# RWKV chain ahead of attention in the first block of a two-block float32 kernel, with sigmoids written as tanh

## The reference

```python
h = rms_norm(x, pre_norm_gain)
proj = h @ w_in                                   # 1024 -> 8832 columns
# attention: 3 groups of 8 heads (q, k, v of 1536 columns each), dilations 1, 4, 16
num, den, mx = dilated_group_attention(q_g, k_g, v_g, bias_g, window, dilation)
o_attn = sum(w * num) / sum(w * den)              # merged over the groups: 512 columns
y_attn = (o_attn * silu(z_attn)) @ w_up_attn      # 512 -> 1024
# RWKV: r, k, v of 512 columns, w_low and a_low of 64 columns
pr = pr + (pr_prev - pr) * shift_mix              # token shift
w_log = -softplus(-(w0 + tanh(w_low) @ w_up)) - 0.5
decay = exp(-exp(w_log))                          # = exp(-e^-0.5 * sigmoid(...))
a = sigmoid(a0 + a_low @ a_up)
kk = normalised per head(k * k_k);  k = k * (1 + (a - 1) * k_a)
S = S * decay + (S @ -kk) (kk * a)^T + v k^T;  y = S @ r     # per token, 8 heads of 64
o_rwkv = group_norm(y) + bonus
y_rwkv = (o_rwkv * silu(z_rwkv)) @ w_up_rwkv      # 512 -> 1024
merged = sigmoid(g_attn) * y_attn + sigmoid(g_rwkv) * y_rwkv
x = x + rms_norm(merged @ w_out, post_norm_gain)
# then block two and the experts: 3 matrices of 1024 x 2816 for each of 16 experts
```

## Time and profile before

| | us |
|---|---|
| median of 3 runs | 2008.4 |
| the profiled execution, its own time | 2008.44 |
| its span in the trace | 2006.5 |
| start of the first projection tile | 17.20 |
| end of the 30 q, k, v tiles | 141.84 |
| first logits to last values of attention | 145.3 to 254.1 |
| end of the chain's last matmul | about 433.8 |
| start of `out1` | 486.55 |
| experts' stretch, DMA-bound | from about 780 to the end |

### The profile page before, as it was taken

One profiled execution on the slowest core, in us unless ns is written; L12 is line 12 of the kernel. 1 busy time (PEld: TensorE's weight loads), 2 busy tenths in 40 slices (PEclk: granted clock), 3 DMA queues, 4 the chain that ended last, 5 costly groups with the idle time before them and its releaser, 6 DMA issues.

```text
span 2006.5 us, 22014 instructions
## 1 busy us (share of the span) xinstructions
PE 1447.0 (72%) x10234; PEld 799.2 (40%) x10234; DVE 538.2 (27%) x696; ACT 162.8 (8%) x322; POOL 12.7 (1%) x25
## 2 busy tenths in 40 slices
PE   7999998887999879665656655656566656565655
PEld 6857877775485444221212222212122222121221
DVE  1005576854633532111111111011111110111112
ACT  2112130001210220000000000000000000000001
POOL 0000000001000000000000000000000000000000
PEclk9999998868999978787777877877878777778778
DMA  8342231114231659999999999999999999999996
GB/s 310 142 148 91 75 117 44 44 43 161 84 126 44 272 230 430 429 431 431 431 435 433 433 430 431 430 432 431 432 434 434 430 432 430 430 432 433 433 432 266
DMA packets 49342, 629.86 MB, mean 314 GB/s; under 512 B 2746, under 2 KB 3869, under 8 KB 36388
## 3 DMA queue, kind: packets, MB, share of 16 engines
q1 hardware_dynamic: 46464, 619.19, 73.3%
q0 software_dynamic: 2224, 8.17, 1.2%
q10 hardware_dynamic: 564, 1.10, 0.2%
HBM read 627.37 MB, written 1.09 MB: 313 GB/s over the span
## 4 chain that ended last, share of the span: by engine, by line
DMA 53%; PE 38%; DVE 7%; ACT 1%; issue 1%; ACTq 0%; DVEq 0%
DMA arena<-in_w_down 18%; DMA arena<-in_w_gate 18%; DMA arena<-in_w_up 16%; PE psum L793 10%; PE psum L1258 6%; PE psum L1300 3%; PE psum L1092 3%; PE psum L795 2%; PE psum L1016 1%; PE psum L1155 1%; DVE arena L1453 1%; PE psum L919 1%; PE psum L812 1%; PE psum L841 1%; PE psum L1006 1%
## 5 line engine op out<-in xcount | busy, mean ns | idle before, releaser
L1258 PE MATMUL psum<-arena 128*32 128x352 f32 x4096 | 415.5, 571 | 273.3 <-DMA arena<-in_w_gate 137.2
L1300 PE MATMUL psum<-arena 128*32 128x512 f32 x1408 | 236.7, 788 | 183.3 <-DMA arena<-in_w_down 180.3
L1258 PEld LDWEIGHTS psum<-arena 128*32 128x32 f32 x4096 | 152.1, 133 | 529.4 <-issue 221.5
L793 PE MATMUL psum<-arena 128*128 128x256 f32 x976 | 226.4, 389 | 1.0 <-ACT arena L540 0.6
L1300 PEld LDWEIGHTS psum<-arena 128*32 128x32 f32 x1408 | 65.7, 135 | 350.0 <-issue 249.9
L793 PEld LDWEIGHTS psum<-arena 128*128 128x128 f32 x976 | 186.2, 194 | 33.3 <-issue 4.8
L1804 DVE TENSOR_TENSOR arena<-psum,arena 128x1024 f32<-128x1024 f32 x30 | 36.7, 1225 | 408.6 <-PE psum L1310 408.6
L1787 DVE COPY arena<-psum 128x256 f32<-128x256 f32 x16 | 6.8, 425 | 303.2 <-PE psum L1286 303.2
L1796 DVE TENSOR_TENSOR arena<-psum,arena 128x704 f32<-128x704 f32 x16 | 14.3, 892 | 259.6 <-PE psum L1258 259.6
L743 ACT ACTIVATE arena<-psum 128x1024 f32<-128x1024 f32 x15 | 15.4, 1025 | 780.3 <-PE psum L1300 780.3
L1792 DVE RECIPROCAL arena<-arena 128x704 f32<-128x704 f32 x16 | 72.9, 4554 | 0.5
(11 more groups left out here) (368 smaller groups left out, 1147.9 us busy)
## 6 DMA issues: line engine op xcount, KB each, us to landing
arena<-in_w_gate SPq DMA_DIRECT2D x32, 5632.0 KB, 46.4
arena<-in_w_up SPq DMA_DIRECT2D x31, 5632.0 KB, 45.9
arena<-in_w_down SPq DMA_DIRECT2D x30, 5632.0 KB, 47.5
arena<-in_w_in SPq DMA_DIRECT2D x24, 2048.0 KB, 8.2
arena<-in_w_out SPq DMA_DIRECT2D x4, 2048.0 KB, 7.9
arena<-in_w_down SPq DMA_DIRECT2D x2, 2816.0 KB, 27.0
arena<-in_w_up SPq DMA_DIRECT2D x1, 4224.0 KB, 12.2
arena<-bias_rows POOLq DMA_DIRECT2D x3, 1024.0 KB, 8.7
```

The lines of the kernel that those rows point to most:

```text
L793: last = mm(o, block_of(blk)[:, k, c * P:c * P + P], rhs[:, k, :], start=(k == 0), stop=(k == KC - 1))
L1258: last = mm(psum[32 * j:32 * j + CAP, b + n, 0:HALFQ], XC[e % 2][:, k, :], region(o, HALFQ), start=(k == 0), stop=(k == KC - 1))
L1300: last = mm(psum[32 * g:32 * g + CAP, 4 + n, :], HT[:, i, :], region(spot(pos), 512), start=(i < 4), stop=(i >= FPP - 4))
```

## The change

The order of the first block is turned round. The blocks of weights are loaded, and the tiles computed, in the order low, k, r, v of RWKV, then q, k, v of attention, then the two silu gates, then the four merge gates. With it:

- The decay and key preparation runs beside the tiles of r, k, v and of q. Whole tiles, two per level, stand among the `pairs`; 3 whole and 8 half tiles (tiles 34 to 40) stand in the chain; six tiles cover the group norm, and four more cover its gating.
- Attention comes last. The 16 merge-gate tiles stand among its units, none behind the last one. The gating of a head (`gated`) is done on DVE straight from PSUM, where ACT copied it before.
- `w_up_rwkv` comes ahead of `w_up_attn`. The merge is one DVE operation per product and one add per k, on which `out1` waits step by step (`mg_ready`).
- Sigmoids are 0.5 * (1 + tanh(x / 2)): Tanh on ACT, and the rest folded into operations of two scalars on DVE. The eight reciprocals go, that of the key norm stays. The factor 0.5 of the merge is in the copy of `out1`.
- The last level's second set of `pairs`, which nothing read, is gone.
- POOL: the three bias loads wait for the last level (`T1_mm` 5). Of the ten loads after the group norm, `dist` and `lam` wait for the last logits and `w3` for the last maximum of attention, since their places in memory are in use until then.
- Buffers are placed anew.

```diff
-        blocks = [(f"q{i}", in_cols(w_in, 512 * i)) for i in range(3)]
+        blocks = [("low", in_cols(w_in, OFF_LOW, P))]
+        blocks += [(f"rkv{i}", in_cols(w_in, OFF_RWKV + 512 * i)) for i in (1, 0, 2)]
+        blocks += [(f"q{i}", in_cols(w_in, 512 * i)) for i in range(3)]
...
             def bank_of(j):
-            if j < ATT_TILES:
-                return j % 4
-            return 6 if PREP_TILE <= j < NORM_TILE and (j - PREP_TILE) % 2 else 7
+            if j < 2:
+                return 2 + j
+            return 6 + j % 2 if j < G_TILE else 7
...
+            pool.wait_ge(S["T1_mm"], 5)
             for g in range(NG):
...
+            pool.wait_ge(S["neg_max"], NU)
+            pool.dma_start(w3[0:64, :], A["filt_w3"]).then_inc(S["f_in"], 16)
...
-                    act.activation(dst, src, ACT.Exp, scale=-1.0).then_inc(S["proj_evac"], 1)
+                if j >= G_TILE:
+                    act.activation(dst, src, ACT.Tanh, scale=scale).then_inc(S["proj_evac"], 1)
...
             for lev in range(5):
                 pe.wait_ge(S["MM_done"], 2 * lev + 2 if lev else 3)
                 pairs(0, mOff, mMT).then_inc(S["T1_mm"], 1)
-                project(LEVEL_TILE + lev, 0, 4)
+                project(24 + 2 * lev)
                 pe.wait_ge(S["T1_done"], lev + 1)
                 pe.wait_ge(S["MM_done"], 2 * lev + 3)
                 pairs(2, mM, mT1).then_inc(S["MM_mm"], 1)
-                pairs(4, mT1, mM).then_inc(S["MM_mm"], 1)
-                project(LEVEL_TILE + lev, 4, 8)
+                if lev < 4:
+                    pairs(4, mT1, mM).then_inc(S["MM_mm"], 1)
+                project(25 + 2 * lev)
...
+            solve(0)
+            project(34)
+            step(0)
+            project(35)
+            state_parts(1)
+            project(36)
+            solve(1)
+            project(37, 0, 4)
+            step(1)
+            project(37, 4, 8)
+            state_parts(2)
+            project(38, 0, 4)
...
+            for j in range(41, 47):
+                project(j)
+            pe.wait_ge(S["gn_done"], 1)
...
+            for n in range(NU):
+                turned(n)
+                if n + 2 < NU:
+                    logits(n + 2)
+                if n + 1 < NU:
+                    project(G_TILE + 1 + n)
+                values(n)
...
-            link(V.tensor_scalar(LD, LD, 1.0, None, ALU.add))
-            link(V.reciprocal(LD, LD))
-            link(V.tensor_scalar(LD, LD, -E_HALF, None, ALU.mult))
+            link(V.tensor_scalar(LD, LD, -0.5 * E_HALF, -0.5 * E_HALF, ALU.mult, ALU.add))
...
-                if lev == 0:
-                    gate_group(0)
```

More of the change, by code:

```diff
@@ new lines, in _ @@
+            evac(0)
+            act.wait_ge(S["low_in"], 1)
+            act.activation(prT[0:64, 12, :], prT[0:64, 12, :], ACT.Tanh).then_inc(S["low_t"], 1)
+            evac(1)
+            evac(2)
+            act.wait_ge(S["low_mm"], 1)
+            for f in range(FT):
+                act.activation(LD[:, f, :], psum[:, f // 2, (f % 2) * T:(f % 2) * T + T], ACT.Tanh, scale=0.5,
+                               bias=small[:, 16 + f:17 + f])
+                last = act.activation(AA[:, f, :], psum[:, 2 + f // 2, (f % 2) * T:(f % 2) * T + T], ACT.Tanh, scale=0.5,
+                                      bias=small[:, 20 + f:21 + f])
@@ L543, in _ @@
+            evac(39)
+            evac(40)
+            evac(41)
+            act.wait_ge(S["mean_in"], 2)
+            act.activation(small[:, 64:80], small[:, 64:80], ACT.Sqrt).then_inc(S["root_in"], 1)
+            for j in range(42, 47):
+                evac(j)
+            act.wait_ge(S["gn_done"], 1)
+            for j in range(47, G_TILE):
                 evac(j)
@@ new lines, in _ @@
+            project(2)
+            pe.wait_ge(S["low_t"], 1)
+            pe.wait_ge(S["proj_evac"], 2)
+            for f in range(FT):
+                mm(psum[:, f // 2, (f % 2) * T:(f % 2) * T + T], lowW[0:64, f * P:f * P + P], prT[0:64, 12, :], start=True, stop=True)
+                last = mm(psum[:, 2 + f // 2, (f % 2) * T:(f % 2) * T + T], lowW[64:128, f * P:f * P + P], prT[64:128, 12, :], start=True, stop=True)
+            last.then_inc(S["low_mm"], 1)
+            for j in range(3, 9):
+                project(j)
@@ new lines, in _ @@
+            pe.wait_ge(S["sq_ready"], 1)
+            for f in range(FT):
+                last = mm(psum[:, 4 + f // 2, (f % 2) * T:(f % 2) * T + T], BLK1, TMP[:, f, :], start=True, stop=True)
+            last.then_inc(S["norm_mm"], 1)
+            for j in range(9, 18):
+                project(j)
+            pe.wait_ge(S["sq_ready"], 2)
+            pe.wait_ge(S["norm_sqrt"], 1)
+            for a in range(TT):
+                for f in range(FT):
+                    last = mm(psum[:, 4, a * 8 + 2 * f:a * 8 + 2 * f + 2], CS[:, f, a * P:a * P + P], small[:, 24 + 2 * f:26 + 2 * f], start=True, stop=True)
@@ L800, in _ @@
+            solve(3)
+            project(40, 0, 4)
+            step(3)
+            project(40, 4, 8)
+            for j in range(41, 47):
+                project(j)
+            pe.wait_ge(S["gn_done"], 1)
+            for a in range(TT):
+                for f in range(FT):
+                    last = nc.tensor.transpose(psum[:, 4 + a, f * P:f * P + P], Y[:, a, f * P:f * P + P], ident)
+                last.then_inc(S["or_mm"], 1)
+            for j in range(47, G_TILE):
                 project(j)
```

631 lines of the change are left out of this document (280 added, 351 removed).

## The result

The changed kernel takes **1937.6 us** (median of 4 runs, 1936.4 to 1940.2), the kernel before took 2008.2 beside it. The ratio is 0.9652, with a 95% interval of 0.964 to 0.9664. That is 70.6 us less, where 69.3 were forecast. The profiled execution took 1938.71 us, its span was 1936.9 us.

The account below looks back on a forecast made before the run. Idle PE and its low clock ahead of `out1` bound the kernel, expert weights following behind. PE's list summed to 415.9 us plus 1.3 of waits: `out1` at 417.2, 69.3 earlier, so 1939.1 us; range 1934 to 1958.

Parts of the forecast that it names:

- Where the gain comes from: Ahead of `out1`: 37.9 us of idle PE and 32.8 us of low clock to be saved; unchanged behind it.
- Runs of tiles, tiles alone, the sets of the levels: PE's first block: 30 tiles in runs 105.6 us, 15 tiles alone 54.9 us, the levels' sets 29.7 us.
- The chain: RWKV chain of 416 records on PE: 17.2 us by a solve's ratio of 0.56, with 30.6 us as upper bound.
- `low`: Product on PE at the start of the first block: 2.97 us.
- the bonus and the turning: PE products: 7.68 us busy at clock 0.62, so 4.8 us at full clock.
- The preparation: DVE's decay and key work ends at 73.2 us; PE asks behind tile 17 at 84.5: 11 us of slack.
- rival 5: Preparation late by more than its 11 us of slack, each us counting once, under 5 expected: 1944 us; chance 0.03.
- The new waits: PE waits 0.5 us at the start of attention and 0.8 at its end; Tanh and Exp share a table.
- Rival 1: Clock stays low in the chain, tiles among it double, together +53: 1992 us; chance 0.06.
- Rival 2: Half clock from the gram stage to the chain's end, some 175 us doubling: up to 2110 us; chance 0.03.
- Rival 3: Expert weight stream starts by something outside the first block, gain not passed on: near 2008 us; chance 0.02.
- Rival 4: `w3` held until DVE's merge work is over, landing some 8.6 us behind; `out1` near 427: 1949 us; chance 0.02.

Follow-up runs that it names:

- The run that asks after tile 12: Changed kernel with tiles 13 to 17 moved behind the bonus and the turning, so PE asks for the preparation earlier: 1949.0 us, ratio 0.9707.
- the bare chain: Changed kernel with tiles 34 to 40 computed right behind the RWKV chain and not in it: 1954.3 us, ratio 0.9728.
- the run with the late load: Changed kernel with GpSimd issuing the load of `w3` only when the up product of the merge is done: 1950.4 us, ratio 0.9714.
- The run of the order alone: Changed kernel with its sigmoids as Exp, add and reciprocal again, eight reciprocals back on DVE: 1984.1 us, ratio 0.9877.

## Why the prediction was right

The time was 1.5 us from the median, and 400.0 us were forecast for the stretch from the first tile to `out1` (417.2 - 17.2), where 399.97 were measured. That is closer than its terms deserve. By its steps:

- **Where the gain comes from.** Confirmed. Idle PE of 37.9 us became 0.8, the clock is 1.00 in every stretch, and from `out1` to the end it is 1519.1 us where it was 1520.0.
- **Runs of tiles, tiles alone, the sets of the levels.** Attention with its start and end took 106.4 us (106.4 forecast), the levels' products 29.6 (29.7), Gram 5.04 (5.0), the up products 27.9 (27.8). The runs of tiles took 104.4, and 105.6 were forecast.
- **The chain.** This term was mis-sized: 17.2 us by the ratio of one solve, 19.4 measured (4 solves of 1.07, 4 steps of 2.93 to 2.99 and 3 state parts of 1.08). The ratio of one solve, 0.56, was taken for all of the chain. The solve did take 1.07 us, so the steps and state parts are what it doesn't fit. Three terms that were too high made up for it, by luck: `low` 1.9 us and not 3.0, the runs of tiles 1.2 us less, and the bonus and the turning 4.4 us and not 4.8.
- **The preparation.** It ended at 73.07 us (forecast 73.2), and PE asked at 83.98 (84.5). The run that asks after tile 12 puts a price on a slack used up: more than the "each us counts once" of rival 5, since 6.2 us of wait took 10.1 us up to `out1`. The 11 us of slack themselves were right.
- **The new waits.** 0.17 us at the start of attention and 0.65 at its end, where 0.5 and 0.8 were forecast. Tanh and Exp share a table: ACT loads one at 255.0 us, and none again until 386.4, behind the last exponent of the 16 units.
- **Rival 1**, the low clock in the chain: it did not come, and the bare chain shows how near it is. Without tiles the clock was 0.50 for most of the chain. There the prediction's argument was too weak: it held that PE must be idle "for us at a time" for the clock to fall, and waits of under 0.8 us were enough.
- **Rival 2**, half clock most of the block: no sign of it. **Rival 3:** the gain was passed on in full.
- **Rival 4**, `w3` late: it landed 6.0 us after its issue, and after 5.7 to 6.0 us in the nine other traces of the new order with the load in this place. The rule named there (SBUF — State Buffer, "SBUF: two separate sides", in the Trainium skill) is neither borne out nor refuted by the runs. The load was issued at 379.0 us, behind the last maximum, and DVE then stood idle until 382.2, so this issue did not test it. The slow landing of 8.2 us came with DVE idle too. The 8.6 us of the earlier trace rows were for a load with a DVE operation of 2.28 us beside its issue and nine other loads of POOL around it. Had the rival come true, it would have cost about what the rival said: 12.8 us in the run with the late load.

What the prediction did not see is that its two ingredients depend on each other. It added idle time and clock, and never asked what the order would be worth with the reciprocals in place. The run of the order alone shows that I would have been wrong there by 16 us, on the side of too much cover: an operation of 6.55 us on DVE does not hide in attention, whose units need DVE every few us.

## What to carry to other kernels

Where an engine waits again and again for short steps of another, put independent work into the waits, and count the gain as idle time plus clock; in this chain the clock was more than twice the idle time. Sum such a change along the engine's list and then ask at each wait how much slack is left: the subtraction gave the waits for DVE here to within 0.5 us, but the one wait for DVE that was made to come cost 1.6 times its length. Long operations in the queue of an engine that others ask often cost more once an order is tight: without the reciprocals the old order was 31 us faster and the new one 46.

## What the runs showed that I had not expected

- Useless work made a kernel faster: 14 added products in the bare chain, 7.4 us of PE, took 11.0 us off the median (1954.3 to 1943.3) and 8.0 us off the stretch from the first tile to `out1` (413.0 to 405.0).
- Waits of 1.3 us, one in each 7.1 us, left the clock at 1.00. In the bare chain the clock fell after three waits of 0.74 to 0.79 us within 7.2 us, and it stayed at 0.50 with one of 0.8 and one of 0.2 in each 9.6 us.
- The first tile starts anywhere between 16.5 and 17.9 us in executions of the same front part (the new order's), which is more than some of the edits tried here are worth.
- One reciprocal of 128 x 1024 takes 6.56 us on DVE and two of 128 x 512 take 3.35 us each, so splitting it costs 0.15 us.
